# Quarter products for all but one pair of the second block's up projections, with three of four weight sums made by adding transfers

## The reference

```python
def conv_glu_ffn(x, w_up, conv_w, conv_b, w_down):
    u = x @ w_up                      # 1024 -> 2 * 2816
    u = lax.conv_general_dilated(u, conv_w...)  + conv_b   # causal, 3 taps, per feature
    gate, val = jnp.split(u, 2, axis=-1)
    return (jax.nn.silu(gate) * val) @ w_down
```

## Time and profile before

| | us |
|---|---|
| three timed executions | 1493.63, 1498.30, 1500.53 |
| their median | 1498.3 |
| the profiled execution | 1495.52 |
| its span in the trace | 1493.7 |
| TensorE busy in it | 1436.2 (96%) |
| VectorE | 926.6 (62%) |
| ScalarE | 328.6 (22%) |
| GpSimd | 25.9 (2%) |
| mean TensorE clock granted | 0.985 of full |

### The profile page before, as it was taken

The page is one execution under the profiler, slowest core; times in us unless marked ns, Lnnn a source line. Parts: engine busy times, 40 slices in busy tenths (PEclk is TensorE's granted clock), DMA queues, the critical chain, the costliest instruction groups (busy, mean ns, idle before and its releaser), DMA issues.

```text
span 1493.7 us, 30779 instructions
## 1 busy us (share of the span) xinstructions
PE 1436.2 (96%) x13094; PEld 1308.1 (88%) x13094; DVE 926.6 (62%) x1862; ACT 328.6 (22%) x657; POOL 25.9 (2%) x32
## 2 busy tenths in 40 slices
PE   7999999989999999998889999999999899999997
PEld 6889788989999987777887998999999678999997
DVE  2288332337885553476653788787687546887875
ACT  1134102231000121420112122221100662322211
POOL 0130000000001000000000000000000000000000
PEclk9999999999999999999999999999999979999999
DMA  9444244237545423321000344445545002454452
GB/s 349 148 140 145 95 149 146 73 128 227 171 168 167 164 71 113 113 71 45 5 4 3 107 149 155 154 143 174 184 151 170 29 1 96 159 169 156 156 173 82
DMA packets 56276, 190.49 MB, mean 128 GB/s; under 512 B 9009, under 2 KB 11185, under 8 KB 55762
## 3 DMA queue, kind: packets, MB, share of 16 engines
q1 hardware_dynamic: 50480, 180.67, 36.1%
q10 hardware_dynamic: 5666, 7.92, 1.6%
HBM read 187.51 MB, written 1.05 MB: 126 GB/s over the span
## 4 chain that ended last, share of the span: by engine, by line
PE 90%; DVE 5%; ACT 3%; issue 1%; DMA 0%; DVEq 0%; ACTq 0%; SPq 0%; PEldq 0%
PE ps L1835 90%; DVE arena L1639 1%; DVE arena L1667 1%; DMA ring<-in_stream 0%; ACT L1363 0%; ACT arena L1366 0%; DVE rs L2303 0%; ACT arena L1363 0%; ACT L1366 0%; ACT arena L1359 0%; ACT arena L1361 0%; DVE arena L1666 0%; DVE arena L1770 0%; DVE arena L2370 0%; ACT L2124 0%
## 5 line engine op out<-in xcount | busy, mean ns | idle before, releaser
L1835 PE MATMUL ps<-arena,ring 128*128 128x128 f32 (+6 forms) x4720 | 806.9, 323 | 16.1 <-DMA ring<-in_stream 8.3
L1835 PEld LDWEIGHTS ps<-arena,ring 128*128 128x128 f32 x4720 | 708.3, 192 | 85.8 <-issue 16.5
L1835 PE MATMUL ps<-arena 64*64 64x64 f32 (+9 forms) x7100 | 597.0, 259 | 24.6 <-DVE arena L1667 8.3
L1835 PEld LDWEIGHTS ps<-arena 128*128 128x128 f32 (+3 forms) x7100 | 532.9, 164 | 60.7 <-issue 28.8
L843 DVE TENSOR_TENSOR arena<-ring 128x512 f32<-128x512 f32 x104 | 71.8, 690 | 122.3 <-PE ps L1835 89.0
L830 ACT COPY arena<-ps 128x128 f32<-128x128 f32 (+2 forms) x76 | 20.3, 267 | 363.7 <-PE ps L1835 363.7
L1835 PE MATMUL ps<-arena,consts 16*128 16x16 f32 (+11 forms) x384 | 83.7, 349 | 6.1 <-DVE arena L1791 1.8
L1616 DVE SCALAR_TENSOR_TENSOR arena<-arena,cols 128x271 f32<-128x271 f32 (+3 forms) x176 | 82.8, 491 | 9.8 <-ACT arena L1281 6.7
L1835 PEld LDWEIGHTS ps<-arena,consts 128*128 128x128 f32 (+3 forms) x384 | 60.1, 185 | 23.7 <-issue 4.2
L1281 ACT ACTIVATE arena<-arena,cols 128x272 f32<-128x272 f32 (+1 forms) x88 | 48.8, 601 | 122.8 <-DVE arena L1548 68.9
L845 DVE TENSOR_TENSOR arena<-arena,ring 128x512 f32<-128x512 f32 x104 | 72.8, 700 | 3.6
(11 more groups left out here) (278 smaller groups left out, 904.5 us busy)
## 6 DMA issues: line engine op xcount, KB each, us to landing
ring<-in_stream SPq DMA_DIRECT2D x342, 512.0 KB, 3.8
consts<-in_consts ACTq DMA_DIRECT2D x1, 1580.0 KB, 8.8
arena<-in_x_t ACTq DMA_DIRECT2D x1, 1024.0 KB, 5.9
arena<-in_mem_t ACTq DMA_DIRECT2D x1, 1024.0 KB, 4.9
res<-in_x_t ACTq DMA_DIRECT2D x1, 1024.0 KB, 14.3
out_t<-arena SPq DMA_DIRECT2D x4, 256.0 KB, 2.5
arena<-in_g ACTq DMA_DIRECT2D x1, 640.0 KB, 5.9
arena<-in_w ACTq DMA_DIRECT2D x2, 256.0 KB, 4.6
```

Source lines behind the costliest of these rows:

```text
L1835: return nc.tensor.matmul(out, lhs, rhs, start=start, stop=stop)
```

## The change

In both layers pairs 1 to 21 are computed in seven products; only pair 0 stays whole. The two sets of banks are given in the other order, and the waits for the whole pairs go.

The weight sums of pair 1 are made as before. For pairs 2 to 21 they are made so:

- ScalarE copies a21 into the buffer of s1 and -a21 into that of s3 (`begin_first_and_third_sum`), for pairs 2 and 3 ahead of the loop and for pair m + 3 in turn m, right behind `keep_first_product`;
- GpSimd issues two transfers that read quarters a22 and a11 again from the weights in HBM, in runs of 512 bytes, and add them onto these buffers (`add_from_stream`), counted in `s1_s3_added`;
- VectorE waits for both and makes s2 = s1 - a11 (`second_weight_sum`), in turn m for pair m + 2;
- ScalarE copies -s2 into the buffer of s4 (`begin_fourth_sum`), in turn m between the first taps and the silu, and a third transfer adds a12 to it, counted in `s4_added`, for which TensorE waits ahead of product 3.

The sums of consecutive pairs use three buffers by turns in place of two.

```diff
--- before.py
+++ after.py
@@ -364,19 +364,33 @@
                               ("upq", Seven(FIRST["up"], P, [4], (3, 0), WIDE_UP, UH // 2, FF // 2, -UH, True), 1),
                               ("down", Seven(FIRST["down"], P, [4] * 4, (4, 0), SPLIT, 0, 4, 0, True), 4),
                               ("rw_o", Seven(FIRST["rw_o"], T2, [4], (0, 4), SPLIT, 1, 4, GB, True), 1),
-                              ("ffa_up", Seven(FIRST["ffa_up"], T2, [4], (0, 4), WIDE, 1, F2, GB, True, 2), 1),
+                              ("ffa_up", Seven(FIRST["ffa_up"], T2, [4], (4, 0), WIDE, 1, F2, GB, True), 1),
                               ("ffa_down", Seven(FIRST["ffa_down"], T2, [4, 4, 3], (4, 0), SPLIT, 0, 4, 0, True), 6),
                               ("sb_k", Seven(FIRST["sb_k"], T2, [4], (4, 0), WIDE, 1, 4, GB, True), 1),
                               ("sb_v", Seven(FIRST["sb_v"], T2, [4], (4, 0), WIDE, 0, 4, GB, False), 0),
                               ("sb_q", Seven(FIRST["sb_q"], L2 // 2, [4], (4, 0), WIDE, 0, 4, GB, False), 1),
                               ("sb_o", Seven(FIRST["sb_o"], L2 // 2, [4], (0, 4), SPLIT, 1, 4, GB, True), 1),
-                              ("ffb_up", Seven(FIRST["ffb_up"], L2 // 2, [4], (0, 4), WIDE, 1, F2, GB, True, 2), 1),
+                              ("ffb_up", Seven(FIRST["ffb_up"], L2 // 2, [4], (4, 0), WIDE, 1, F2, GB, True), 1),
                               ("ffb_down", Seven(FIRST["ffb_down"], L2 // 2, [4, 4, 3], (4, 0), SPLIT, 0, 4, 0, True), 6)):
             y.pair0, y.group0, y.sums0 = n_pairs, n_groups, n_sums
             SEVEN[name] = y
             n_pairs, n_groups = n_pairs + len(y.pairs()), n_groups + len(y.groups) * len(y.pairs())
             n_sums += sums
 
+        def sums_of(name, i, g):
+            y = SEVEN[name]
+            at = y.group(i, g) % 2
+            if name in ("ffa_up", "ffb_up"):
+                first = y.group(1, 0) % 2
+                return (WSUM[name][first], WSUM["ffn"][1], WSUM[name][1 - first])[(i - 1) % 3]
+            return WSUM[name][at]
+
+        def added_on_the_way(name, i):
+            return name in ("ffa_up", "ffb_up") and i >= 2
+
+        def turns_of_sums(name, i):
+            return (F2 // 2 - 1) * (name == "ffb_up") + i // 2
+
         def product_at(y, i, p, more=1):
 
             bank, at = y.place[p]
@@ -388,6 +402,8 @@
             return upper[:, :, 0, :], upper[:, :, 1, :], lower[:, :, 0, :], lower[:, :, 1, :]
 
         SHARED = {"sb_v": 0}
+        sums_begun = sem("sums_begun")
+        s1_s3_added, s4_added = [[sem(f"{x}_added{n}") for n in range(2)] for x in ("s1_s3", "s4")]
         products, w_summed, p1_kept, x_summed = sem("products"), sem("weights_summed"), sem("p1_kept"), sem("x_summed")
 
         def arrived(eng, b, it=None):
@@ -739,8 +755,8 @@
                 pe.sem_inc(ev[up], GB)
                 pe.wait_ge(ev[before], GB + 6)
                 for m in range(F2):
-                    if m % 2:
-                        if m == 3:
+                    if m:
+                        if m == 2:
                             pe.wait_ge(rooted, 10 + i)
                         seven_products(pe, mm, up, only=m)
                         continue
@@ -749,8 +765,6 @@
                         arrived(pe, b)
                         if s == 1:
                             pe.wait_ge(ev[before], GB + 8)
-                        elif m:
-                            pe.wait_ge(ev[up], GB + s - 3)
                         for k in range(KT):
                             if s == 0:
                                 pe.wait_ge(res_scaled, 8 * i + k + 1)
@@ -800,7 +814,7 @@
                     second()
                 for g, n in enumerate(y.groups):
                     b, done = y.block(i, g), 4 * y.group(i, g)
-                    s1, s2, s3, s4 = [WSUM[name][y.group(i, g) % 2][:, x] for x in range(4)]
+                    s1, s2, s3, s4 = [sums_of(name, i, g)[:, x] for x in range(4)]
                     a11, a12, a21, a22 = w_quarters(b)
                     w_of = {1: a11, 2: a12, 3: s4, 4: a22, 5: s1, 6: s2, 7: s3}
                     arrived(pe, b)
@@ -813,6 +827,8 @@
                     for p in ORDER:
                         if p in (6, 7, 3):
                             pe.wait_ge(w_summed, done + {6: 2, 7: 3, 3: 4}[p])
+                            if p == 3 and added_on_the_way(name, i):
+                                pe.wait_ge(s4_added[i % 2], 16 * turns_of_sums(name, i))
                         bank = y.place[p][0]
                         for l in range(n):
                             last = mm(product_at(y, i, p), w_of[p][:, l, :], x_of[p][:, 4 * g + l, :],
@@ -846,6 +862,51 @@
             tt(s3, a11, a21, ALU.subtract).then_inc(w_summed, 1)
             dve.wait_ge(w_summed, done + 2)
             tt(s4, a12, s2, ALU.subtract).then_inc(w_summed, 1)
+
+        def second_weight_sum(dve, tt, name, i):
+            y = SEVEN[name]
+            s1, s2 = [sums_of(name, i, 0)[:, x] for x in range(2)]
+            arrived(dve, y.block(i) + 1)
+            dve.wait_ge(s1_s3_added[i % 2], 32 * turns_of_sums(name, i))
+            tt(s2, s1, w_quarters(y.block(i))[0], ALU.subtract).then_inc(w_summed, 4)
+
+        def begin_first_and_third_sum(act, f, name, i):
+            y = SEVEN[name]
+            sums, a21 = sums_of(name, i, 0), w_quarters(y.block(i))[2]
+            arrived(act, y.block(i))
+            if i >= 4:
+                act.wait_ge(used, y.block(i - 2))
+            f(sums[:, 0], a21, ACT.Copy)
+            f(sums[:, 2], a21, ACT.Copy, scale=-1.0).then_inc(sums_begun, 1)
+
+        def begin_fourth_sum(act, f, name, i):
+            y = SEVEN[name]
+            sums = sums_of(name, i, 0)
+            act.wait_ge(w_summed, 4 * y.group(i, 0) + 4)
+            f(sums[:, 3], sums[:, 1], ACT.Copy, scale=-1.0).then_inc(sums_begun, 1)
+
+        def add_from_stream(pool, name):
+            y = SEVEN[name]
+            n0 = 2 * (F2 - 2) * (name == "ffb_up")
+
+            def quarter(b, c):
+                return stream[b].rearrange("p (k c m) -> p k c m", k=4, c=2)[:, :, c, :]
+
+            def first_and_third(i):
+                b, at = y.block(i), i % 2
+                pool.wait_ge(sums_begun, n0 + (i - 1 if i < 4 else 2 * i - 4))
+                for x, src in ((0, quarter(b, 1)), (2, quarter(b + 1, 0))):
+                    pool.dma_start(out=sums_of(name, i, 0)[:, x], in_=src, accum_op=ALU.add).then_inc(s1_s3_added[at], 16)
+
+            def fourth(i):
+                pool.wait_ge(sums_begun, n0 + min(2 * i - 1, i + F2 - 3))
+                pool.dma_start(out=sums_of(name, i, 0)[:, 3], in_=quarter(y.block(i) + 1, 1),
+                               accum_op=ALU.add).then_inc(s4_added[i % 2], 16)
+            first_and_third(2)
+            for i in range(2, F2):
+                if i + 1 < F2:
+                    first_and_third(i + 1)
+                fourth(i)
 
         def x_sums(link, tt, name, at=slice(None)):
             b11, b12, b21, b22 = [x[:, at, :] for x in x_quarters(name)]
@@ -1271,15 +1332,21 @@
             wc = COLS["conv_w"] + layer * 3 * 2 * F2 + 2 * 2 * F2
             bc = COLS["conv_b"] + layer * 2 * F2
             m0 = layer * (2 + F2)
+            begin_first_and_third_sum(act, f, name + "_up", 2)
+            begin_first_and_third_sum(act, f, name + "_up", 3)
 
             for m in range(F2):
-                if m % 2:
+                if m:
                     keep_first_product(act, name + "_up", m)
+                    if m + 3 < F2:
+                        begin_first_and_third_sum(act, f, name + "_up", m + 3)
                 for s in (2 * m, 2 * m + 1):
                     act.wait_ge(ev[name + "_up"], GB + s + 1)
                     act.wait_ge(ffm, m0 + m + 1)
                     f(cu[:, s % 4, :], uu[:, s % 4, :], ACT.Identity, scale=cols[:, wc + s:wc + s + 1],
                       bias=cols[:, bc + s:bc + s + 1]).then_inc(ffc, 1)
+                if m + 2 < F2:
+                    begin_fourth_sum(act, f, name + "_up", m + 2)
                 act.wait_ge(conv_done, layer * 2 * F2 + 2 * m + 1)
                 f(cu[:, (2 * m) % 4, :], cu[:, (2 * m) % 4, :], ACT.Silu).then_inc(ffs, 1)
 
@@ -1598,15 +1665,15 @@
 
             up, down = name + "_up", name + "_down"
             for m in range(F2):
-                if m % 2:
+                if m:
                     quads_scaled(up, m, uu[:, (2 * m) % 4:(2 * m) % 4 + 2, :])
-                    if m + 2 < F2:
-                        weight_sums(dve, tt, up, m + 2, 0)
                 else:
                     for s in (2 * m, 2 * m + 1):
                         dve.wait_ge(used, b + s + 1)
                         tt(uu[:, s % 4, :], gps(3 + 4 * (s % 2), width), rs[:, 0:width], ALU.mult).then_inc(ev[up], 1)
-                if m >= F2 - 2:
+                if m < F2 - 2:
+                    second_weight_sum(dve, tt, up, m + 2)
+                else:
```

(2 more changed lines are left out.)

## The result

| | us |
|---|---|
| kernel before, median of the runs beside this one | 1499.4 |
| changed kernel, median of four (1521.6 to 1541.1) | 1537.0 |
| ratio, with 95% interval | 1.023 (1.018 to 1.029) |
| forecast | 1482.1, range 1477 to 1524 |

A forecast was written before the change was run, and what follows sets the result against it. The up stages were taken as bound by TensorE's matmuls; 16.2 us less matmul time, all other work hidden beside it, gave 1498.3 - 16.2 = 1482.1 us, range 1477 to 1524.

The forecast's parts named there:

- The matmul time removed: TensorE, both up stages: ten pairs per layer go from whole to quarter products, 0.85 and 0.77 us each, 16.2 us less.
- VectorE's turn: VectorE's work per pair in the up stages: 5.98 us against TensorE's 6.49, 92%, so it fits.
- GpSimd's issue: Issuing three adds per pair on GpSimd: 1.2 us each taken, bounds 0.33 to 1.89, limit 2.16 us.
- the forecast's second rival: Up stages: GpSimd's issue over 2.16 us each becomes the bound, about 1527 us; chance 0.12.
- Room on the DMA engines: Up stages, per pair: adds 2.1 us of an engine, with the weight stream 4.7 to 5.3 of 6.49 us, so it fits.
- the low end of my bounds: DMA price of a 512 B adding run: 22 ns, half a 1 KB packet's 45 ns.
- the mark of being wrong: Forecast declared wrong if an adding run costs over 35 ns of an engine or an issue over 2.1 us.
- the main rival: Up stages: adding runs cost as 1 KB packets, so DMA engines become the bound, 1503 to 1527 us; chance 0.24.
- the two rows: Profile rows behind the DMA price: final stores' 1 KB packets at 45 ns, early stream's 4 KB packets at 164 ns.
- Time from issue to landing: Adds in the up stages: 3.8 us to land, as ring blocks of twice the size, against 7.2 to 7.7 us of room.
- start-up stalls: Stage starts: a few us, counted in the likeliest case's spread of 1477 to 1488 us.
- its signs: Profile after: DMA share 0.95 or more, adds landing 8 us and more after issue, VectorE's single sum and TensorE waiting for DMA.

The follow-up runs named there:

- e1: The change without the weight sums of pairs 2 to 21 and their copies, adds and waits (pair 1's sums reused); 1485.4 us, ratio 0.990.
- e2: The change with its 120 transfers only copying, not adding, on the same software queue (sums wrong); 1480.6 us, ratio 0.990.
- e5: The change with plain copies issued by ScalarE on its hardware queue in place of adds and ScalarE's copies (sums wrong); 1483.5 us, ratio 0.989.
- e10: The change with VectorE making s1 and s2, and one 512 KB add per pair in 4 KB runs for s3 and s4; 1497.1 us, ratio 0.997.
- e4: The change without transfers or ScalarE copies: GpSimd computes s1, s3 and s4, VectorE s2; 1579.2 us, ratio 1.055.
- e7: The change with only s1 and s3 by adds, in 512 B runs, VectorE making s2 and s4; 1527.2 us, ratio 1.019.

## Why the prediction was wrong, point by point

**The matmul time removed** was right: 16.2 us said, 14.6 us of stage in e1, e2 and e5, and 0.989 to 0.990 in time (15 to 17 us).

**VectorE's turn**, 5.98 us, held: in e2 the turn from 894.00 to 899.64 is 5.64, with its share of input sums 6.1, and TensorE was not held up. It grew only by the waits that stood in it.

**GpSimd's issue**, taken as 1.2 us, measured so (two in 2.46 us, one in 1.22); GpSimd was busy in 73 of 163 us, and the forecast's second rival is out:

```profile
903.44 2.46 POOL L899 DMA_DIRECT2D arena<-in_stream  x2 [2.97 <-ACT arena L880]
906.58 1.22 POOL L903 DMA_DIRECT2D arena<-in_stream  x1 [0.68 <-ACT arena L886]
```

**Room on the DMA engines** is the step that failed. I priced an adding run at 22 ns by the bytes of a copy, the low end of my bounds; it measured 64 ns, above the 35 ns that I had named as the mark of being wrong and even above the 45 ns of the main rival. By my own sum 96 of them are 6.2 us and with the stream's 3.2 us 9.4, and the rival decided from 37 to 43 ns. The argument for the low end, that time went by bytes in the two rows, was fair for copies (28 ns in e5) and said nothing on adding: both rows were of packets that copy. The pace was 7.9 us (333.7 over 42 turns) and not 9.4, as packets of the two queues overlap: 9.4 over 7.9 is 1.19, the summed share of the two queues.

**Time from issue to landing**: 3.8 us was taken from ring blocks that had the queue to themselves; the adds took 7.1 us in the median and up to 11.7. At the start of each stage four adds go out at once and VectorE waited 5.5 us for the second of them; I had allowed a few us for start-up stalls.

**The main rival** named the mechanism and its signs and had the chance of 0.24. The share was over 0.95 and TensorE waited for DMA; the landing was 7.1 us in the median where it said 8 and more. Its time of 1503 to 1527 and the range's end at 1524 were too low. Of the 60.3 us between the stages of the change and of e2, TensorE's waits in its quarter products are 39.8:

```profile
L1902 PE MATMUL ps<-arena 128*128 128x136 f32 x1344 | 181.1, 283 | 17.3 <-DMA arena<-in_stream 16.3 <-DVE arena L871 1.0
...
L1902 PE MATMUL ps<-arena 128*128 128x130 f32 x1248 | 165.3, 282 | 22.5 <-DMA arena<-in_stream 21.5 <-DVE arena L871 1.0
```

The other 20.5 us are matmuls that ran slower, nearly all from the lower clock, which no case of the forecast had: by the windows above, 4% of 163 us and 6% of 165 us, it took some 16 us in them (an estimate). The four runs of the change agree: 1521.6 us at a mean clock of 0.981, the other three 1533 to 1541 at 0.970 to 0.973.

**What stays open**: why an adding packet costs 30 ns and 68 ns per KB, whether for the second read or the adder itself; what a packet of 512 B costs on the software queue without an add; and how much of an add's late landing is the load. No experiment separated them.

## What to carry to other kernels

Price a transfer that computes from a transfer that computes: adding cost 1.8 to 2.3 times the engine time of a copy here, and its packets stayed as short as its runs. Ask of every "free" helper what share of its resource is already taken: at 0.46, adds that took another 0.8 did not fit. If adds are used at all, lay the source out in long runs, merge them, and let nothing but the last consumer wait for them; and count, for waits of TensorE of 2 us and more, that slow matmuls may follow. Where VectorE's turn has no slack, a wait at the start of the stage is paid in full at its end.

## What the runs showed of the hardware

- DMA packets by kind, mean engine time each: copy of 512 B 28 ns; add of 512 B 64 ns (67 from SBUF), of 2 KB 166 ns, of 4 KB 325 ns (e10, 42.8% of 2080 us over 2736; 30 ns and 68 ns per KB would make it 302). A software queue merged eight copied runs of 512 B into one packet of 4 KB, and no added ones.
- GpSimd's issue took 1.2 us for an add of 512 runs, 0.86 us for one of 128 (e10) and 0.75 us for a plain copy of 512 runs (e2).
- VectorE's tap over two SBUF operands took two to three times as long beside GpSimd's two-operand work in e4 (mean 1533 and 961 ns for the two taps against 0.49 us). Its sums and copy-outs kept their times, but they mostly fell where GpSimd was idle.
- TensorE's clock stood at 0.53 after an idle time of 3.65 us, and at 1.00 in e7 from 870 to 1010 us, where its waits were 1.6 us at most. In between both were seen in the change: after 1.97 us the 8 records took 1.72 us, after 2.24 us 1.17 us (full speed), and after 3.08 us full speed too.
